# Three seams of a hybrid decoder block: feature-tile projections at the head, the last gate slab in a result bank, statistics in quarters

## The reference

```python
h = layer_norm(concat([meta, x]), emb_ln_g, emb_ln_b)
z = h @ w_in + b_in            # qa, ka, va, qb, kb, vb, fb, ga, gb
oa = sliding_window_attention(qa, ka, va, sinks, rel_table)   # 8 heads of 64, window 128
ob = forgetting_attention(qb, kb, vb, log_sigmoid(fb))        # 8 heads, causal, decayed
y = (sigmoid(ga) * (oa @ w_pa) + sigmoid(gb) * (ob @ w_pb)) @ w_o
h = layer_norm(2 ** 0.25 * h + y, ln1_g, ln1_b)
y = peer_ffn(h, ...)           # 8 heads choose 16 of 16384 experts each, u and v rows per expert
out = layer_norm(2 ** 0.25 * h + y, ln2_g, ln2_b)[16:]
```

## Time and profile before

| | us |
|---|---|
| median of 3 runs | 1705.8 (1704.66 to 1707.39) |
| the profiled execution, its own time | 1718.52 |
| its span, first to last instruction | 1716.4 |
| PE busy in the span | 1653.8 (96%) |
| DVE busy in the span | 1339.5 (78%) |
| ACT busy in the span | 735.2 (43%) |

### The profile page before, as it was taken

The page is one execution under the profiler, slowest core; times in us unless marked ns, Lnnn a source line. Parts: engine busy times, 40 slices in busy tenths (PEclk is TensorE's granted clock), DMA queues, the critical chain, the costliest instruction groups (busy, mean ns, idle before and its releaser), DMA issues. The chain is left out here.

```text
span 1716.4 us, 26821 instructions
## 1 busy us (share of the span) xinstructions
PE 1653.8 (96%) x9808; PEld 1523.3 (89%) x9808; DVE 1339.5 (78%) x2848; ACT 735.2 (43%) x1288; POOL 452.1 (26%) x314
## 2 busy tenths in 40 slices
PE   5999999999979999999999999999999999999996
PEld 4897776577768899999999999999999999999996
DVE  5434554644467888999999989967989999999898
ACT  4214544333143354566766754434333333333331
POOL 0000000000001105133132432332544545457550
PEclk9999999889989999999999999999999999999998
DMA  5731111012214459699899999999999999999991
GB/s 167 198 95 55 39 48 38 25 49 86 74 61 155 129 157 379 217 341 336 269 316 340 353 307 332 341 398 392 382 400 410 407 408 408 407 402 409 407 404 78
DMA packets 185441, 438.47 MB, mean 255 GB/s; under 512 B 17832, under 2 KB 102000, under 8 KB 182880
## 3 DMA queue, kind: packets, MB, share of 16 engines
q1 hardware_dynamic: 73872, 227.43, 36.3%
q0 software_dynamic: 44080, 161.06, 25.5%
q10 hardware_dynamic: 67360, 48.28, 8.5%
HBM read 380.57 MB, written 56.13 MB: 254 GB/s over the span
## 5 line engine op out<-in xcount | busy, mean ns | idle before, releaser
L464 PE MATMUL psS<-hT_lo,hi 128*128 128x368 f32 (+2 forms) x1504 | 518.4, 345 | 4.6 <-DVE hT_lo L1021 3.9
L465 PE MATMUL psS<-hT_hi,lo 128*128 128x368 f32 (+2 forms) x1504 | 510.1, 339 | 0.0
L466 PE MATMUL psS<-hT_hi,hi 128*128 128x368 f32 (+2 forms) x1504 | 508.5, 338 | 0.0
L455 DVE TENSOR_TENSOR lo<-raw,hi 128x1024 fp32r<-128x1024 f32 x323 | 394.6, 1222 | 119.7 <-ACT hi L451 110.5
L451 ACT ACTIVATE hi<-raw 128x1024 fp32r<-128x1024 f32 x323 | 340.0, 1053 | 177.4 <-PE psS L466 124.0
L569 POOL DMA_INDIRECT gat<-in_u_rows,idx x144 | 214.7, 1491 | 393.1 <-DVE gat L1195 214.8
L464 PEld LDWEIGHTS psS<-hT_lo,hi 128*128 128x128 f32 x1504 | 283.8, 189 | 30.8 <-issue 15.6
L466 PEld LDWEIGHTS psS<-hT_hi,hi 128*128 128x128 f32 x1504 | 283.9, 189 | 13.4
L465 PEld LDWEIGHTS psS<-hT_hi,lo 128*128 128x128 f32 x1504 | 283.8, 189 | 11.1
L569 POOL DMA_INDIRECT gat<-in_v_exp,idx x144 | 220.8, 1533 | 233.9 <-DVE gat L1195 151.4
L766 ACT ACTIVATE act_hi<-act_t 128x368 fp32r<-128x368 f32 x128 | 65.6, 513 | 278.9 <-DVE act_t L1246 264.0
(11 more groups left out here) (303 smaller groups left out, 2630.1 us busy)
## 6 DMA issues: line engine op xcount, KB each, us to landing
raw<-in_u_exp SPq DMA_DIRECT2D x128, 512.0 KB
raw<-in_v_exp SPq DMA_DIRECT2D x128, 512.0 KB
gelu_dram<-gelu ACTq DMA_DIRECT2D x128, 184.0 KB
gates_dram<-gates ACTq DMA_DIRECT2D x92, 256.0 KB
gel_in<-gelu_dram SPq DMA_DIRECT2D x128, 184.0 KB
raw<-in_w_merge SPq DMA_DIRECT2D x24, 512.0 KB
gate_even<-gates_dram SPq DMA_DIRECT2D x8, 1472.0 KB
gate_odd<-gates_dram SPq DMA_DIRECT2D x8, 1472.0 KB
```

The source lines that it names most:

```text
L455: nc.vector.tensor_tensor(lo[:, n % RING, :], raw[:, n % RING, :], hi[:, n % RING, :].bitcast(F32), ALU.subtract).then_inc(lo_done, 1)
L464: nc.tensor.matmul(out_ap, w_h, x_l, start=start, stop=False)
L465: nc.tensor.matmul(out_ap, w_l, x_h, start=False, stop=False)
L466: return nc.tensor.matmul(out_ap, w_h, x_h, start=False, stop=stop)
```

## The change

Three seams are altered; the sums computed stay the same.

1. **Head.** `N_EARLY = 3`: after feature tile k has been turned, TensorE multiplies tile k - 1 into projection slabs 0, 1 and 2, which collect in banks of `psT` and `psO`. The `lo` of these slabs is made ahead of all `hT_lo`. The turns of tile 0 start as each token block is normalised. The product for the bias table moves from the end of the turns to the start of slab 5, and DVE's part of it behind the emptying of slab 5.
2. **Attention and mix.** `TILES` moves eight tiles (one slab) from steps 14, 15 and 32 to 38 to steps 44 to 47; that slab, number 13, collects in bank `psO[:, 0, :]`. `oT_lo` is placed four steps after the block's end instead of three. The two gate slabs of the last m run between the attention and the first mix slab. The first output slab waits for `m_lo` tile by tile.
3. **Statistics.** Turned sums are collected two tiles at a time: four quarters in changing banks, each with four statistics of 256 columns. TensorE's wait for the first statistics is now ahead of tile 6.

```diff
-TILES = [4] * 16 + [2] * 16 + [3, 3, 2, 2, 2, 2, 2, 0] + [0] * 8
+TILES = [4] * 14 + [3] * 2 + [2] * 16 + [2, 2, 2, 2, 1, 1, 0, 0] + [0, 0, 0, 0, 2, 2, 2, 2]
+        def sum_bank(c, t):
+            return banks[((4, 5), (6, 7), (1, 3), (4, 5))[c][t // 2]]
+        def gate_bank(v):
+            return psS[:, v % 2, SEQ:] if v < N_GATE - 1 else psO[:, 0, :]
...
 DVE
+            for n in range(N_EARLY):
+                split_lo(dve, n)
             for k in range(KT):
...
-                if k < AHEAD:
-                    split_lo(dve, k)
...
+                if n == N_EARLY + 2:
+                    dve.wait_ge(bias_in, 64)
+                    dve.wait_ge(w_mm, 1)
+                    V.tensor_tensor(wrow[:, 0, :], psO[0:HEADS, 0, 0:3 * P], wrow[:, 1, :], ALU.add).then_inc(w_done, 1)
...
-                w = block_ended(s - 3)
+                w = block_ended(s - 4)
...
+            def quarter_stats(c):
                 dve.wait_ge(r_turned, c + 1)
                 for t in range(NBLK):
-                    ins = V.bn_stats(stats1[:, t, 6 * c:6 * c + 6], banks[4 + t])
+                    ins = V.bn_stats(stats1[:, t, 6 * c:6 * c + 6],
+                                     sum_bank(c, t)[:, t % 2 * (SEQ // 2):(t % 2 + 1) * (SEQ // 2)])
...
 TensorE
+            for k in range(KT + 1):
+                if k < KT:
...
+                    for t in range(NBLK):
+                        if k == 0:
+                            pe.wait_ge(norm_done, t + 2)
+                        turn(psS[:, k % 2, t * P:(t + 1) * P], xin[:, t, k * P:(k + 1) * P], ident)
...
+                if k >= 1:
+                    j = k - 1
+                    if j == 0:
+                        pe.wait_ge(lo_done, N_EARLY)
+                    pe.wait_ge(hT_lo_done, k)
+                    for n in range(N_EARLY):
+                        halves = [slice(0, HALF), slice(HALF, COLS)] if n == 0 else [slice(0, SEQ)]
+                        for b, cols in enumerate(halves):
+                            out_ap = banks[4 + b][:, 0:HALF] if n == 0 else banks[5 + n]
+                            last = slab(n, n, out_ap, lambda k: hT_hi[:, k, cols], lambda k: hT_lo[:, k, cols],
+                                        [(j, j)], ends=(j == 0, j == KT - 1))
...
+                        if v == N_GATE - 1:
+                            pe.wait_ge(o_hi_done, 2 * NBLK - 1)
+                            pe.wait_ge(o_lo_done, 2 * NBLK - 1)
...
+            for j in range(2):
+                n = FIRST_MERGE + N_GATE + j
+                pe.wait_ge(lo_done, n + 1)
+                slab(n, n % RING, psS[:, 1, j * SEQ:(j + 1) * SEQ], tokens, tokens_lo, all_k).then_inc(slab_used, 1)
             pe.wait_ge(o_lo_done, 2 * NBLK)
...
-                if k == KT // 2:
+                if k == KT - 2:
                     pe.wait_ge(r_stats_done, 1)
...
-                pe.wait_ge(m_lo_done, KT)
+                for k in range(KT):
+                    if m == 0:
+                        pe.wait_ge(m_lo_done, k + 1)
+                    last = slab(n, n % RING, psS[:, m % 2, 0:SEQ], lambda k: m_hi[:, k, :], lambda k: m_lo[:, k, :],
+                                [(k, k)], ends=(k == 0, k == KT - 1))
```

More of the change, by code:

```diff
@@ L42 @@
 N_PROJ = 19
+N_EARLY = 3
 N_MERGE = 24
@@ L644, in _ @@
                     act.wait_ge(mix_done, m - 1)
-                if m < KT - 1:
-                    split_hi(act, FIRST_MIX + m + AHEAD)
-                    for j in range(2):
+                split_hi(act, FIRST_MIX + m + AHEAD)
+                for j in range(2):
+                    if m < KT - 1:
                         nc.scalar.activation(gate[:, m % 2, j, :], gate_input(2 * m + j), ACT.Sigmoid).then_inc(gate_done, 1)
[L649 to L656, removed]
+                    else:
+                        act.wait_ge(slab_used, FIRST_MERGE + N_GATE + j + 1)
+                        nc.scalar.activation(gate[:, m % 2, j, :], psS[:, 1, j * SEQ:(j + 1) * SEQ], ACT.Sigmoid,
+                                             bias=bcol[:, N_PROJ + 8 * j + m:N_PROJ + 8 * j + m + 1]).then_inc(gate_done, 1)
                 act.wait_ge(mix_done, m + 1)
@@ L860, in halves @@
                     return v.rearrange("p (b c) -> p b c", b=2)
-                ps = halves(psS[:, n % 2, :])[:, :, 0:HALF]
+                whole = psT[:, :] if n == 0 else psS[:, n % 2, :]
+                square = banks[5 + n] if 1 <= n < N_EARLY else psS[:, n % 2, 0:SEQ]
+                ps = halves(whole)[:, :, 0:HALF]
                 if n == 0:
@@ L897, in _ @@
             dve.wait_ge(ck_in, 16)
-            for s in range(N_STEPS + 4):
+            for s in range(N_STEPS + 5):
                 last_step = 1 <= s <= N_STEPS
@@ L961, in _ @@
                                     oT_hi[:, w // NBLK, :, cols].bitcast(F32), ALU.subtract).then_inc(o_lo_done, 1)
+            for j in range(2):
+                split_lo(dve, FIRST_MERGE + N_GATE + j + AHEAD)
             for m in range(KT):
[L965 to L968, removed]
+                split_lo(dve, FIRST_MIX + m + AHEAD)
+                dve.wait_ge(slab_used, FIRST_MIX + m + 1)
                 dve.wait_ge(gate_done, 2 * m + 2)
@@ L993, in _ @@
                                          ALU.add))
+                if m >= 3 and m % 2 == 1:
+                    quarter_stats((m - 3) // 2)
                 dve.wait_ge(slab_used, FIRST_OUT + m + 1)
@@ L1352, in _ @@
             pe.wait_ge(cst_in, 48)
[L1354 to L1362, removed]
@@ L1364, in _ @@
             pe.wait_ge(xT_done, KT)
-            for n in range(N_PROJ):
+            for n in range(N_EARLY, N_PROJ):
                 pe.wait_ge(lo_done, n + 1)
-                if n >= 2:
+                if n >= N_EARLY + 2:
                     pe.wait_ge(evacuated, n - 1)
+                if n == N_EARLY + 2:
+                    pe.wait_ge(bias_in, 64)
+                    mm(psO[0:HEADS, 0, 0:3 * P], relb[:, :], buck[:, :], start=True, stop=True).then_inc(w_mm, 1)
                 if 1 <= n <= 4 or 7 <= n <= 10:
@@ L1374, in _ @@
                         half = slice(b * HALF, (b + 1) * HALF)
-                        if n == 0 and b == 0:
-                            for k in range(KT):
-                                pe.wait_ge(hT_lo_done, k + 1)
-                                slab(n, 0, psS[:, 0, 0:HALF], lambda k: hT_hi[:, k, half], lambda k: hT_lo[:, k, half],
-                                     [(k, k)], ends=(k == 0, k == KT - 1))
-                            continue
                         last = slab(n, n % RING, psS[:, n % 2, b * SEQ:b * SEQ + HALF], lambda k: hT_hi[:, k, half],
@@ L1514, in _ @@
                 pe.wait_ge(lo_done, n + 1)
-                pe.wait_ge(m_lo_done, KT)
                 if m >= 2:
                     pe.wait_ge(r_done, m - 1)
-                slab(n, n % RING, psS[:, m % 2, 0:SEQ], lambda k: m_hi[:, k, :], lambda k: m_lo[:, k, :],
-                     all_k).then_inc(slab_used, 1)
+                for k in range(KT):
[3 more added lines that the diff above has]
+                                [(k, k)], ends=(k == 0, k == KT - 1))
+                last.then_inc(slab_used, 1)
                 if m >= 1:
```

67 lines of the change are left out of this document (34 added, 33 removed).

## The result

The changed kernel takes 1686.1 us (median of 4 runs, 1683.5 to 1688.6), the kernel before 1705.6 us (4 runs in the same set, 1704.7 to 1707.4): a ratio of 0.9885, 95% interval 0.9867 to 0.9902. That is 19.5 us faster. The forecast was 1674, so it has the side right and the gain 12 us too large. The range, 1666 to 1691, holds the time.

What follows compares the result with a forecast made beforehand. TensorE, busy 96% of the span, was taken as the bound; its idle holes and half clock in the first 480 us counted. Terms -3.4 - 15.1 - 13.4 = -31.9 us took the median 1705.8 to 1674 us, range 1666 to 1691.

Steps and rivals of the forecast that it cites:

- Part 1: Head: early slab work between turns gains 4.1 us, the exposed table product costs 0.7; -3.4 us in sum.
- rival of a head at half clock: Head: turns between slab work keep the clock down, head ends at 60.1, total 1689 us; chance 0.16.
- rival on the slow side: Bias table late: its store, slowed by slab loads, delays the attention; at 95 us, 1712 us; chance 0.04.
- Part 2: Attention to seam: probability waits and seam hole go, tail keeps full clock, some new wait; -15.1 us in sum.
- the 0.5 us of new wait: Attention steps 38 and 39, left without tiles: TensorE would wait 0.5 us more where a slab's lo falls in.
- rival of a tail at half clock without a hole: Attention's tail: clock falls in steps 38 to 43 though no hole is left, total 1689 us; chance 0.13.
- Part 3: Mix, output, statistics: two holes with their half clock go and the last statistics get shorter; -13.4 us in sum.
- The sum: All edits together against the profiled execution: -31.9 us, from 1718.5 to 1686.6.
- its own list: Signs of being wrong: a 0.50 stretch over 10 us before 470, or a changed length from spread to end.
- Carried over to the runs: Whole kernel: both kernels' profiled executions stand 12.7 us above their medians alike, so 1705.8 becomes 1674 us.
- the plain runs never had the tail's fall: Attention's tail: without the profiler its hole may not lower the clock; gain 10.7 us less, 1685 us; chance 0.08.
- The forecast's main case: Whole kernel: the forecast of 1674 us holds, within 1667 to 1680 us; chance 0.57.

Runs made afterwards that it cites:

- its copy: The kernel before, unedited, run again: five runs from 1706.0 to 1709.6 us and five from 1716.5 to 1718.8.
- part 1 alone: The kernel before with only the head's edits (early slabs between turns, table product at slab 5): 1706.5 us, ratio 0.9999.
- part 3 alone: The kernel before with quarter statistics and the first output slab waiting for m_lo tile by tile: 1697.6 us, ratio 0.9941.
- part 2: The kernel before with tiles moved to steps 44 to 47, slab 13's bank changed, oT_lo later, gate slabs at the seam: 1701.0 us, ratio 0.9939.

## Why the prediction was right, and where it was wrong

**Part 1, forecast -3.4.** At the attention's start it is -2.2 in the kernel after and -3.0 alone. Slab work began at 21.12 (forecast 21.4), the full clock came at 26.7 (26.5). One tile then takes 2.91 us (turns at 34.64 and 37.55) where 2.75 were put, so slab 3 starts at 45.81 instead of 44.8, against 48.9 before. The rival of a head at half clock is refuted: turns between slab work didn't hold the clock down. The store moved behind the head still took 34.3 us and the read back 7.0 (34.3 and 7.5 in the earlier trace rows), and no compute engine waited for them. Slab loads beside the store came late as before: ACT waited 7.1 and 3.9 us for two of them, near 95 and 100 us, and TensorE did not stop. The rival on the slow side fell too.

**Part 2, forecast -15.1.** Between the attention's start and the first mix slab, less the 11.1 us of moved gate slabs, it is -16.1. Steps with tiles take 4.68 and 4.70 us (4.7), those without 3.20; the 0.5 us of new wait did not come. The rival of a tail at half clock without a hole is refuted by the steps from 304.8 to 322.8: the same 18 us that the rival names, dense, without tiles, and at 1.00.

**Part 3, forecast -13.4.** From the first mix slab to the spread it is 98.6 + 11.1 = 109.7 us against 123.4: -13.7.

**The sum, forecast -31.9.** The spread starts at 452.46 instead of 484.43: -32.0. The remaining 3.1 us of the span's 35.1 came where nothing was edited, among them 1.0 us of waits for gates that the profiled execution of before has and its copy doesn't. By its own list the forecast would be wrong if the part from the spread to the end were not as long as before. It is 1228.8 us against 1232.0, but over the fourteen profiles it lies anywhere from 1228.8 to 1234.4. So one such pair cannot tell, and what the rest is stays open.

**Carried over to the runs: the step that failed.** The forecast let both kernels carry the 12.7 us between the profiled execution and the median alike. They are not an overhead of the profiler. They are the tail's half clock after its hole of 1.78 us. By their times and mean clocks 29 of 72 executions have it and 41 don't. The stretch itself is seen only in the two profiles of the upper level; its absence at the lower level is seen in edited kernels that keep the hole (part 1 alone, part 3 alone) or fill it. The change removes the hole, so the kernel after has no such level (10 executions: nine from 1683.5 to 1688.6, and one of 1692.5 with a clock of 0.993) and its profiled execution carries nothing: 1683.5 against a median of 1686.1. The gain is 32 against the upper level and 32 - 11 = 21 against the lower. From the lower level's 1706.3 this gives 1685.3; measured were 1686.1 and 1685.6. The forecast had this as the rival "the plain runs never had the tail's fall", with 1685 and a chance of 0.08. It was right in its number and nearly in its mechanism; only that it is not the profiler but the execution that decides. What should have raised this rival's chance lay in the numbers before: a profiled execution 0.7% above runs that agree within 0.16%, and a stretch at half clock worth 23.3 x (1 - 3.20/5.92) = 10.7 us, nearly the same amount.

**What was luck.** The forecast's main case, 1667 to 1680 at 0.57, did not come. The measured time also lies near the 1689 of the two rivals at half clock, which the traces refute. So the range holds 1686 because it was drawn wide enough for the rivals. That the result shows a gain of 19.5 is luck of the draw as well: all four of its runs of before are at the lower level, at a chance of (41/72)^4, about 10%.

**The parts in the runs.** The sum holds in the profiles, less so in the medians. Against the lower level, 1706.3, part 1 alone is worth 1.1 us, part 2 5.3 and part 3 9.6, together 16.0; the whole change is worth 20.2. A part of the difference may be clock lost behind holes that one part alone leaves standing, as the 1.7 us at the seam in part 3's profile. The rest was not traced.

## What to carry to other kernels

Before a gain read from one profiled execution is promised for the runs, set the two times beside each other: where they differ by much more than the runs differ among themselves, look for a stretch of low clock of that size, and price the edit with it and without it. A short wait of TensorE has two prices, its own length, and with some chance the half clock behind it; here moving one short VectorE operation by one step was worth 4.9 us against the one level and 15.8 against the other. Where such a hole can't be closed, unread matmuls in it cost nothing that was measured and kept the clock in twelve of twelve runs; look further on too, for the clock may fall behind the next hole instead.

## What the runs showed of the hardware

- The same hole does not do the same each time. Behind 1.8 us of idle the clock stayed at 1.00, fell for a few us (0.72 over 326 to 332), or stood at 0.50 for 22 us of dense work. In the kernels whose normalisation is not filled, the 20 us from the spread on had 0.80 to 0.82 in seven profiles, 0.75 in two and 0.68 to 0.70 in three. A hole of 0.69 us was followed by 0.57 over four us in one profile and 1.00 in another. What decides it was not found.
- The fall outlasts its cause: from 332 to 354 TensorE was busy for 22.00 of 22.00 us, at 0.50 all the time.
- The clock's column reads 1.00 in the head of both kernels while the distances of the matmuls, 0.22 us for 264 columns, show 1.2 GHz until 26.7 us in the kernel after and past 33.9 us in the kernel before.
